# Head 0's projections multiplied while w_mod streams in, in a hybrid attention / HGRN2 / conv-FFN block

## The reference, cut to what matters

```
mod = silu(c) @ w_mod + b_mod                  # w_mod [2048, 12288]; mod = sh1, sc1, g1, sh2, sc2, g2
h = rms_norm(x, pre_mix_norm) * (1 + sc1) + sh1
q_a, k_a, v_a, f_b, q_b, i_b, g_b, gate_a, gate_b = split(h @ w_in)
y_a = sliding_window_sink_attention(q_a, k_a, v_a, sinks) @ w_branch_a    # 16 heads, 4 kv heads
y_b = hgrn2_output(hgrn2_chunkwise(q_b, f_b, i_b, lb), g_b) @ w_branch_b  # 8 heads of 128
x = x + g1 * rms_norm((sigmoid(gate_a)*y_a + sigmoid(gate_b)*y_b) @ w_out)
h = rms_norm(x) * (1 + sc2) + sh2
x = x + g2 * rms_norm((gelu(conv(h @ w_up_a)) * (h @ w_up_b)) @ w_down)
```

## Time and profile before

| | |
|---|---|
| median of three runs | 2963.79 us (2961.75 to 2965.9) |
| profiled execution, span from first to last instruction | 2964.4 us |
| TensorE / VectorE / ACT busy | 96% / 50% / 34% of the span |
| mean DMA rate | 128 GB/s, 379.86 MB |
| mean granted TensorE clock | 0.979 of full |

### The profile page before, as it was taken

How to read it: one execution, slowest core, us unless ns; L and a number is a source line. 1 busy time by engine, 2 the same in 40 slices (tenths; PEclk the granted TensorE clock), 3 DMA queues, 4 the chain that set the end, 5 groups by cost and what they waited for, 6 DMA issues and landing times.

```text
span 2964.4 us, 36879 instructions
## 1 busy us (share of the span) xinstructions
PE 2841.2 (96%) x13149; PEld 2367.2 (80%) x13149; DVE 1483.6 (50%) x2012; ACT 1020.3 (34%) x1320; POOL 31.2 (1%) x65
## 2 busy tenths in 40 slices
PE   3699999999999999999989999999999999999997
PEld 3578888888778888878868888888888887888886
DVE  6826777777876666553253333333333333333334
ACT  4224444444532222222243333333333332223222
POOL 1010000000000000000000000000000000000000
PEclk8789999999999999999999999999999999999999
DMA  8943222222457777764333333333333334323222
GB/s 272 298 127 86 79 79 79 79 79 79 132 158 225 218 222 225 210 208 161 99 128 94 98 99 92 99 96 95 99 93 98 98 93 149 98 93 100 95 96 99
DMA packets 451825, 379.86 MB, mean 128 GB/s; under 512 B 20252, under 2 KB 376992, under 8 KB 448928
## 3 DMA queue, kind: packets, MB, share of 16 engines
q1 hardware_dynamic: 438624, 353.61, 39.5%
q0 software_dynamic: 2816, 16.80, 1.5%
q10 hardware_dynamic: 10304, 8.39, 0.9%
HBM read 368.25 MB, written 10.50 MB: 128 GB/s over the span
## 4 chain that ended last, share of the span: by engine, by line
PE 89%; DVE 5%; DMA 3%; issue 2%; ACT 1%; SPq 0%; DVEq 0%; ACTq 0%
PE acc_bank L451 23%; PE acc_bank L453 23%; PE acc_bank L452 23%; DMA raw<-in_w_mod_dram 2%; PE two_banks L453 2%; PE two_banks L451 2%; PE two_banks L452 2%; PE bank_pb L451 1%; PE bank_pb L452 1%; PE bank_tb L453 1%; PE bank_ta L453 1%; PE bank_pb L453 1%; PE bank_ta L451 1%; PE bank_tb L451 1%; PE bank_ta L452 1%
## 5 line engine op out<-in xcount | busy, mean ns | idle before, releaser
L426 DVE TENSOR_TENSOR w_lo<-raw,w_hi 128x1024 fp32r<-128x1024 f32 x474 | 579.7, 1223 | 1289.3 <-ACT w_hi L421 1289.3
L421 ACT CAST w_hi<-raw 128x1024 fp32r<-128x1024 f32 x474 | 498.2, 1052 | 1554.3 <-PE acc_bank L453 1005.7
L451 PE MATMUL acc_bank<-h_hi,w_hi 128*128 128x512 f32 x2576 | 1019.7, 396 | 3.9 <-DVE w_lo L426 3.9
L453 PE MATMUL acc_bank<-h_hi,w_lo 128*128 128x512 f32 x2576 | 1009.6, 392 | 0.0
L452 PE MATMUL acc_bank<-h_lo,w_hi 128*128 128x512 f32 x2576 | 1009.4, 392 | 0.0
L451 PEld LDWEIGHTS acc_bank<-h_hi,w_hi 128*128 128x128 f32 x2576 | 488.6, 190 | 103.5 <-DVE w_lo L426 3.9
L453 PEld LDWEIGHTS acc_bank<-h_hi,w_lo 128*128 128x128 f32 x2576 | 487.5, 189 | 103.1
L452 PEld LDWEIGHTS acc_bank<-h_lo,w_hi 128*128 128x128 f32 x2576 | 488.3, 190 | 98.8
L1167 DVE SCALAR_TENSOR_TENSOR acc<-raw,csil,acc 128x512 f32<-128x512 f32 x240 | 180.0, 750 | 12.9 <-DMA raw<-in_w_mod_dram 6.7
L451 PE MATMUL acc_bank<-w_hi,a_hi 128*128 128x512 f32 x258 | 101.0, 392 | 2.8 <-DVE w_lo L426 2.8
L451 PE MATMUL acc_bank<-o_hi,w_hi 128*128 128x512 f32 x256 | 102.5, 400 | 0.8 <-DVE w_lo L426 0.8
(11 more groups left out here) (321 smaller groups left out, 3071.7 us busy)
## 6 DMA issues: line engine op xcount, KB each, us to landing
raw<-in_w_mod_dram SPq DMA_DIRECT2D x192, 512.0 KB, 4.6
raw<-in_w_ffn_up_dram SPq DMA_DIRECT2D x172, 512.0 KB, 3.8
raw<-in_w_in_dram SPq DMA_DIRECT2D x152, 512.0 KB, 4.0
raw<-in_w_ffn_down_dram SPq DMA_DIRECT2D x86, 512.0 KB, 3.7
raw<-in_w_out_dram SPq DMA_DIRECT2D x32, 512.0 KB, 3.8
raw<-in_w_branch_a_dram SPq DMA_DIRECT2D x16, 512.0 KB, 4.7
raw<-in_w_branch_b_dram SPq DMA_DIRECT2D x16, 512.0 KB, 5.3
x_in<-in_x_dram ACTq DMA_DIRECT2D x4, 1024.0 KB, 8.8
```

Source lines behind the costliest of these rows:

```text
L421: act.copy(w_hi[g % SPL][:], raw[n % RAW][:]).then_inc(hi_ready, 1)
L426: dve.tensor_tensor(w_lo[g % SPL][:], raw[n % RAW][:], w_hi[g % SPL][:].bitcast(F32), ALU.subtract).then_inc(lo_ready, 1)
L451: pe.matmul(o, stat[0], mov[0], start=start, stop=False)
L453: return pe.matmul(o, stat[1], mov[0], start=False, stop=stop)
```

## The change

Head 0's ten pieces become eight pieces among the *start pieces* (18 with the eight of k and v), and are multiplied while w_mod comes in. The two blocks i and q of HGRN2 are loaded together, four k-tiles of each to a piece (`iq`), the others (q, f, g) in halves of eight k-tiles. Each piece waits only for the k-tiles of h that it needs. The first half of q, f and g goes to a partial sum in SBUF (`partial`), to which VectorE adds the second half.

w_mod lands in eight slots of its own (`MODS_SLOTS`), not in raw. x goes first in SP's queue; three vectors (c, b_mod, pre_mix_norm) go on ACT's queue and nine on POOL's. The start pieces have four pairs of w_hi and w_lo. The tables of orders say behind which w_mod piece (0 to 63) a start piece's load is issued (LOAD_AFTER) and its w_lo made on VectorE (SPLIT_AFTER), and ahead of which start piece TensorE sums over the partitions (SUM_BEFORE). POOL builds the tables and masks of the mixing behind the stores of k and of v. The memsets of w_mod's sums go, as do the loops over them. Head 1's pieces are written out, the loop over heads covers 2 to 7. The diff, cut to its core:

```diff
-N1 = KV_PIECES + MODS_HEAD
+N1 = P1
+MODS_IN = 8
+START = P1 + HEAD_PIECES
+START_SPL = 4
+START_PIECES = [("kv", 0), ("kv", 1), ("iq", 0),
+                ("kv", 2), ("q", 0), ("kv", 3), ("iq", 1), ("f", 0),
+                ("kv", 4), ("g", 0), ("kv", 5), ("iq", 2),
+                ("kv", 6), ("kv", 7), ("iq", 3), ("q", 1), ("f", 1), ("g", 1)]
+LOAD_AFTER = {9: 0, 11: 1, 14: 2, 20: 3, 23: 4, 26: 5, 30: 6, 38: 7, 42: 8, 45: 9, 48: 10, 52: 11, 55: 12, 58: 13, 61: 14}
+SPLIT_AFTER = {12: 0, 14: 1, 17: 2, 24: 3, 27: 4, 30: 5, 34: 6, 43: 7, 46: 8, 49: 9, 52: 10, 56: 11, 59: 12, 62: 13}
+SUM_BEFORE = {2: 2, 3: 3, 4: 4, 6: 5, 9: 6, 11: 7}
...
 # SP
+            for i in range(TT):
+                sp.dma_start(x_in[:, i, :], x_rows[i]).then_inc(x_landed[i], 16)
...
+            for j in range(MODS_HEAD):
+                s, i = divmod(j, 8)
+                col = (MOD_SC1, MOD_SH1)[s % 2] * P + (s // 2) * 512
+                if j >= MODS_IN:
+                    sp.wait_ge(mod_ops, 2 * (j - MODS_IN) + 2)
+                sp.dma_start(MODS_SLOTS[j % MODS_IN], w_mod_t[:, 2 * i:2 * i + 2, col:col + 512]).then_inc(mod_landed[j % MODS_IN], 16)
+                if j in LOAD_AFTER:
+                    load_start(LOAD_AFTER[j])
...
 # TensorE
+            def iq_piece(g, c):
+                pe.wait_ge(h_ready, 4 * c + 4)
...
+            def half_piece(g, kind, half):
+                pe.wait_ge(h_ready, 8 * half + 8)
+                which = "qfg".index(kind)
+                if half == 0:
+                    if which == 0:
+                        pe.wait_ge(vec_ready, 2)
+                    else:
+                        pe.wait_ge(part_out, which)
...
+            for g, (kind, c) in enumerate(START_PIECES):
+                if g in SUM_BEFORE:
+                    mod_sum(SUM_BEFORE[g], (SC1_SUMS, SH1_SUMS)[SUM_BEFORE[g] % 2])
+                if (kind, c) == ("q", 1):
+                    pe.wait_ge(kv_out, 4)
...
+                pe.wait_ge(lo_ready, g + 1)
...
 # ACT
+            act.wait_ge(xT_ready, KT)
+            split_start(0, 1, 2)
+            modulate_chunk(0)
+            split_start(3, 4, 5, 6)
+            modulate_chunk(1)
+            split_start(7)
+            take_partial(0, 4)
+            split_start(8, 9)
+            modulate_chunk(2)
+            split_start(10)
+            take_partial(1, 7)
+            split_start(11, 12)
+            take_partial(2, 9)
+            split_start(13)
+            modulate_chunk(3)
+            split_start(14, 15, 16)
+            act.wait_ge(multiplied, 14)
             for b in range(4):
                 act.copy(kvT[:, b, :], KV_BANKS[b][:]).then_inc(kv_out, 1)
+            split_start(17)
...
+                        if first and k == 1:
+                            act.wait_ge(v_stored, 8 * 16)
+                            fetch_v(0)
...
+            act.wait_ge(k_stored, 8 * 16)
+            act.wait_ge(temps_ready, 1)
+            fetch_k(0)
 # VectorE
+            for j in range(MODS_HEAD):
+                s, i = divmod(j, 8)
+                ch = s // 2
+                if i == 0 and s >= 2:
+                    dve.wait_ge(mod_summed, s - 1)
+                if j == 8:
+                    dve.wait_ge(root_ready, 1)
+                    dve.reciprocal(rms, rms).then_inc(rms_ready, 1)
                 for half in range(2):
+                    mod_start(j, half)
+                if j == 2:
+                    take_vectors()
+                if ch and s % 2 == 0:
                     if i == 2:
                         columns(ch - 1)
+                    if 3 <= i <= 6:
+                        h_low(4 * (ch - 1) + i - 3)
+                if j in SPLIT_AFTER:
+                    split_lo(dve, SPLIT_AFTER[j], SPLIT_AFTER[j])
...
+                    if first:
+                        dve.wait_ge(multiplied, START)
+                        TTe(gh[:], A[1][:], partial[:, 2, :], ALU.add).then_inc(E["g_ready"], 1)
...
-            head_step(0, P1, N1, 0, False)
```

More of the change, by code:

```diff
@@ L155, in block_kernel, with w_pair, pair_free @@
         w_lo = [sb(f"w_lo{i}", [P, PIECE], F32R) for i in range(SPL)]
+        START_HI = w_hi + [RO[7]["start_hi"][:, i] for i in range(2)]
+        START_LO = w_lo + [RO[7]["start_lo"][:, i] for i in range(2)]
+        def w_pair(g):
+            if g < START:
+                return START_HI[g % START_SPL], START_LO[g % START_SPL]
+            return w_hi[g % SPL], w_lo[g % SPL]
+        def pair_free(g):
+            return g - (START_SPL if g < START else SPL) + 1
         RS = layouts(
@@ L361, in load_kv @@
[L361 to L377, removed]
@@ L381, in head_src @@
+            for g in range(max(LOAD_AFTER.values()) + 1, START):
+                load_start(g)
             def head_src(h, i):
@@ L455, in weights @@
             def weights(g, kt):
-                return piece(w_hi[g % SPL], kt), piece(w_lo[g % SPL], kt)
+                w_h, w_l = w_pair(g)
+                return piece(w_h, kt), piece(w_l, kt)
             def block_piece(g, it, gp, o, mov_hi, mov_lo, k0, first, last, operand=None):
@@ L525, in _ @@
-            t.then_inc(v_turned, 1)
+            def iq_piece(g, c):
+                pe.wait_ge(h_ready, 4 * c + 4)
+                if c == 0:
+                    pe.wait_ge(xT_ready, KT)
+                wh, wl = weights(g, 8)
+                for k in range(4):
+                    kb = 4 * c + k
+                    for b, bank in enumerate((TB, TA)):
+                        mm = three(bank[:], (wh[:, 4 * b + k, :], wl[:, 4 * b + k, :]), (h_hi[:, kb, :], h_lo[:, kb, :]),
+                                   kb == 0, kb == KT - 1)
+                mm.then_inc(multiplied, 1)
@@ new lines, in half_piece @@
+            def half_piece(g, kind, half):
[6 more added lines that the diff above has]
+                        pe.wait_ge(part_out, which)
+                wh, wl = weights(g, 8)
+                bank = SC1 if half == 0 else (A[2], A[0], A[1])[which][:]
+                for k in range(8):
+                    mm = three(bank, (wh[:, k, :], wl[:, k, :]), (h_hi[:, 8 * half + k, :], h_lo[:, 8 * half + k, :]), k == 0, k == 7)
+                mm.then_inc(multiplied, 1)
```

328 lines of the change are left out of this document (174 added, 154 removed).

## The result

The changed kernel takes 2916.68 us (median of 4 runs, 2914.82 to 2918.45), the kernel before 2962.77 (2961.65 to 2965.9, 4 runs taken beside it): a ratio of 0.9843, 95% interval 0.9829 to 0.9857. Forecast were 2919 us, range 2910 to 2934. The profiled execution took 2914.82 us with a span of 2913.1; its rows follow in the order of those of before, and the numbers of their groups are given. The start pieces are the eight of k and v and all ten of head 0 (four `iq`, and two halves each of q, f and g).

A forecast was written before the change was run, and what follows sets the result against it. TensorE was taken as the bound, the end set by head 1's step: moved from 232.7 to 185.7 us, 47.0 gained, 1.4 lost to v's wait, 45.6 net, so about 2919 us, range 2910 to 2934.

The forecast's parts named there:

- scaling of x on ScalarE: At the start, ScalarE scales x once VectorE has made the norm's factor behind w_mod piece 7: from 27.4 us.
- first w_lo starts: On VectorE behind w_mod piece 12, the first start piece's low half waits for w_hi and starts at 49.5 us.
- columns of chunk 1 done: On VectorE, the pace from 50.7 us: w_mod pieces 13 to 34, splits and columns finish at 88.3 us.
- TensorE restarts with kv piece 2: TensorE waits for h from 86 us and restarts at 93.5 us, then being the bound.
- from there to head 1's step: TensorE without waits from kv piece 2: the remaining pieces, four sums and v's transposes take 92.2 us.
- last w_mod operation ends: On VectorE at the end of w_mod's stream: 145 us, five above the DMA floor.
- TensorE's wait for v: Some 20 us into head 1's step, TensorE stalls for the vcur transfer: 1.4 us taken, between 0 and 6.
- The mis-sized term: the queue: The DMA rate while w_mod streams: 0.524 MB at 335 GB/s, taken as 1.58 us a piece.
- the floor of 140 us: Earliest landing of the last of 64 w_mod pieces, with 8 kv and 7 head 0 pieces in the queue.
- Rival (a), the slow queue: While w_mod streams, 294 to 299 GB/s is the ceiling: 1.75 us a piece, time 2929 us; chance 0.13.
- TensorE's slow start: At kv piece 2, the first 5.3 us after the wait run at half clock, 13 slow matmuls.
- The fetch is issued there: In head 1's step, ScalarE issues v's fetch behind its step 1, 17 us in; it lands 20.3 to 21.3 us in.

The follow-up runs named there:

- e3: The changed kernel with four landing slots for w_mod instead of eight: 2928.12 us, ratio 0.9877 to the kernel before.
- e9: The kernel of e5 with four landing slots for w_mod instead of eight: 2918.61 us, ratio 0.9849 to the kernel before.
- e4: The changed kernel with v's fetch issued only after ScalarE's last exponential of step 1 has ended: 2918.08 us, one run.
- e7: The changed kernel with all of head 0's pieces multiplied behind the eight kv pieces: 2941.58 us, ratio 0.9925 to the kernel before.
- e8: The changed kernel with x back on ScalarE's queue and the twelve vectors ahead of w_mod on SyncE's: 2917.06 us, ratio 0.9842 to the kernel before.
- e5: The changed kernel with the edits of e1 and e2 together: 2905.72 us, ratio 0.9804 to the kernel before.
- e1: The changed kernel with VectorE's w_lo of the first three start pieces behind w_mod pieces 18, 19, 20 instead of 12, 14, 17: 2910.09 us.
- e2: The changed kernel with the norm's factor computed on VectorE at w_mod piece 3 instead of 8: 2911.64 us, ratio 0.9828 to the kernel before.
- e11: The kernel of e5 with six landing slots for w_mod instead of eight: 2905.68 us, ratio 0.9803 to the kernel before.

## Why the prediction came out right, step by step

The mechanism held: VectorE set the time up to kv piece 2, TensorE from there. Point by point, forecast and measured:

```
scaling of x on ScalarE                  27.4     28.48
last copy of xT done                     48       48.96
first w_lo starts                        49.5     50.07
columns of chunk 1 done                  88.3     87.9
TensorE restarts with kv piece 2         93.5     93.04
from there to head 1's step              92.2     91.42
last w_mod operation ends                145      143.5
GpSimd's tables and prob done            177.5    175.3
v's stores issued                        184      181.4
head 1's step                            185.7    184.46
TensorE's wait for v                     1.4      0
time                                     2919     2916.7
```

**The mis-sized term: the queue.** I took 1.58 us a w_mod piece from the best 4 us of the trace before (335 GB/s). The changed kernel moves w_mod at 361 to 378 GB/s over whole windows of 20 us, 0.524 MB in 1.39 to 1.45 us, so the floor of 140 us was some 12 us too high (72 pieces by some 0.17). It cost the forecast little since VectorE was the pace anyway: the faster queue only let VectorE's standstill begin at 37.1 instead of 40, and its end was ScalarE's. The trace before could not show the rate: with four slots e3 and e9 run at 314 to 349 from 60 to 100 us. I had also written that the queue would just not run dry before 54 us; it did, from about 49 until past 53, since the slots filled sooner (mean DMA share from 15 to 54 us 0.93, forecast 0.95 or more). Rival (a), the slow queue, had the wrong sign.

The Trainium skill's limit of about 358 GB/s for one core ("DMA: Bandwidth & Descriptors", Specifications), which I set aside for the rows, is passed by these windows, with 378 GB/s over 20 us. The same page of the Trainium skill, in its section Bandwidth, tells of 425 GB/s for one core alone and of about 358 when both cores of a memory domain stream; this kernel runs on one core, and its 378 is above the second and below the first.

**Small terms.** The scaling began 1.1 us later than forecast, and VectorE's work from the first w_lo's end to the columns took 36.6 us (51.3 to 87.9), forecast 37.6; that the two make up for each other is luck. TensorE's slow start was 3 us instead of 5.3, seven slow matmuls instead of 13: about 1.2 us (six by 0.2), of which the stage was shorter by 0.8. The sum itself, with the 0.6 us between span and median taken off as it says, gives 2918.2 and not 2919. The measured time lies 1.5 us below that: the step came 1.2 us earlier, the stall of 1.4 didn't come, and 1.1 went the other way behind the step.

**v's wait did not come.** The step of the prediction that failed is "The fetch is issued there", 17 us into the step, when ScalarE has done its step 1. The fetch stands in ScalarE's list behind the exponentials, but its queue issued it at 199.63 while the engine was still to run the exponential of 201.42; the list's DMA does not wait for the engine's earlier instructions to finish. e4, which makes it wait, gets a wait of 0.79 us. The fetch was 2.4 us later there and the product 0.95, so the changed kernel has some 1.5 us of cover: the stall was near.

**The remainder.** The span shrank by 51.3 us in the two profiled executions, the step by 48.3. Of the 3.0, 1.6 come in one place, behind head 7, where the two traces drift from 48.8 us apart (847.46 and 798.67) to 50.4 (856.45 and 806.02): the granted clock of the kernel before stood at 0.78 from 851 to 857 us, that of the changed kernel at 1.00 in the same work (803 to 807). By the medians the gain is 46.1, 2.2 less than the step's. In the other profiled executions the time is some 1.7 us above the span (2914.82 and 2913.1), which puts the profiled execution of the kernel before at about 2966, the slowest of its runs. Both remainders are of the size by which executions differ, and I take no cause from them.

**Where the 46 us come from**, by the experiments: interleaving head 0 25 (e7 against the changed kernel); of the other 21, 11 to 13 are the slots (e3, e9), x's place in the queue 0 (e8); the last 8 to 10, the rest of the new order (the early splits and the handover without its hole), were not tried apart, and the parts needn't add up exactly. The change left 11 us behind in its own order of VectorE (e5).

## What to carry to other kernels

Find the one instruction after which the bound engine no longer waits, and look at everything ahead of it on the engine that feeds it; here, with eight slots, each microsecond ahead of kv piece 2 was a microsecond of the kernel (e1, e2, e5), and two lines of order gave 11 more. On an in-order engine a piece of work whose input comes late belongs behind work whose input is there: the split of piece 0 stood still for 13 us while the eight slots behind it filled up. Give a stream as many landing slots as cover the time from issue to landing and the time in which the slot is worked on (here six of 1.4 us were enough and four were not), no more, and don't count idle GpSimd as free while VectorE reads two tensors at a time.

## What the runs showed of the hardware

- One core's queue, most of its traffic in 2 KB rows, held 372 to 378 GB/s for 20 us at a time with eight landing slots of 0.5 MB (e5, 20 to 120 us), 350 to 378 with six (e11), and 314 to 341 with four (e9, 20 to 100 us).
- A DMA in ScalarE's list went out 1.8 us before the engine began an exponential that stands ahead of it in the list.
- VectorE's operations with two tensor inputs and GpSimd's excluded each other for whole operations: 0.75 us became 2.84, and GpSimd's 2.8 became 9.79.
- TensorE was granted full clock 3 us after restarting from a wait of 5.83 us; in the kernel before it took 5.3 us at the start of head 0's pieces. Why the two differ isn't shown.
